# Groups of one to four small matrix products between the weight slots of the gate-up stages

## What is computed

```
def _swiglu(h, w_gu, w_down):
    gate, up = jnp.split(h @ w_gu, 2, axis=-1)
    return (jax.nn.silu(gate) * up) @ w_down        # w_down: 2816 x 1024

def _conv_glu_ffn(h, ffn_up, ffn_conv, ffn_conv_bias, ffn_down):
    u = _causal_dwconv(h @ ffn_up, ffn_conv) + ffn_conv_bias
    gate, val = jnp.split(u, 2, axis=-1)
    return (jax.nn.gelu(gate, approximate=True) * val) @ ffn_down
```

## Time and profile before

| what | value |
|---|---|
| median of 2 runs | 1998.72 us |
| lowest, highest | 1992.91, 2004.54 us |
| the profiled execution's own time | 1990.14 us |
| its span, first to last instruction | 1988.3 us |
| TensorE busy | 1886.5 us, 15758 matmuls |
| VectorE, ScalarE, GpSimd busy | 1211.8, 1002.9, 708.1 us |
| mean granted clock of TensorE | 0.974 of full speed |

### The profile page before, as it was taken

How to read it: one execution, slowest core, us unless ns; L and a number is a source line. 1 busy time by engine, 2 the same in 40 slices (tenths; PEclk the granted TensorE clock), 3 DMA queues, 4 the chain that set the end, 5 groups by cost and what they waited for, 6 DMA issues and landing times.

```text
span 1988.3 us, 41005 instructions
## 1 busy us (share of the span) xinstructions
PE 1886.5 (95%) x15758; PEld 1847.9 (93%) x15758; DVE 1211.8 (61%) x1482; ACT 1002.9 (50%) x1312; POOL 708.1 (36%) x595
## 2 busy tenths in 40 slices
PE   6999999999999999999999998997999889979997
PEld 6999999999999999999999997987999789969997
DVE  4545586666556645676665576556774665657755
ACT  5434465454354435555544456455654474546543
POOL 3761211257416621303376102513660005225630
PEclk9999999999999999999999989998999889999998
DMA  6546444456455546344454633222554433214544
GB/s 222 196 148 218 170 148 148 160 187 206 160 199 190 196 165 216 128 149 170 170 202 160 203 134 106 86 86 87 191 189 160 135 106 107 89 60 170 190 153 165
DMA packets 49225, 314.42 MB, mean 158 GB/s; under 512 B 5712, under 2 KB 6864, under 8 KB 19920
## 3 DMA queue, kind: packets, MB, share of 16 engines
q1 hardware_dynamic: 48960, 311.09, 45.5%
q10 hardware_dynamic: 144, 1.69, 0.2%
HBM read 311.71 MB, written 1.05 MB: 157 GB/s over the span
## 4 chain that ended last, share of the span: by engine, by line
PE 67%; ACT 9%; DVE 9%; DMA 7%; issue 4%; POOL 2%; SPq 0%; ACTq 0%; DVEq 0%; POOLq 0%
PE ps L546 17%; PE ps L548 17%; PE ps L547 17%; ACT w_hi L1175 5%; DMA raw<-in_down_dram 5%; DVE w_lo L1656 4%; PE ps L551 3%; PE ps L885 3%; PE ps L553 3%; PE ps L552 3%; DMA raw<-in_in_dram 1%; PE ps L696 1%; PE ps L736 1%; DVE rstd L1662 1%; DVE conv L1982 1%
## 5 line engine op out<-in xcount | busy, mean ns | idle before, releaser
L1656 DVE TENSOR_TENSOR w_lo<-raw,w_hi 128x2048 fp32r<-128x2048 f32 (+1 forms) x322 | 696.1, 2162 | 359.7 <-ACT w_hi L1175 358.3
L546 PE MATMUL ps<-xn,w_hi 128*128 128x256 f32 x2688 | 763.8, 284 | 39.5 <-DVE w_lo L1656 14.4
L547 PE MATMUL ps<-xn,w_hi 128*128 128x256 f32 x2688 | 754.1, 281 | 0.0
L548 PE MATMUL ps<-xn,w_lo 128*128 128x256 f32 x2688 | 754.0, 280 | 0.0
L1175 ACT ACTIVATE w_hi<-raw 128x2048 fp32r<-128x2048 f32 (+1 forms) x322 | 562.6, 1749 | 135.4 <-DMA raw<-in_down_dram 88.1
L546 PEld LDWEIGHTS ps<-xn,w_hi 128*128 128x128 f32 x2688 | 514.6, 191 | 48.1 <-issue 37.1
L547 PEld LDWEIGHTS ps<-xn,w_hi 128*128 128x128 f32 x2688 | 515.1, 192 | 0.7 <-issue 0.5
L548 PEld LDWEIGHTS ps<-xn,w_lo 128*128 128x128 f32 x2688 | 515.4, 192 | 0.0
L546 PE MATMUL ps<-h,w_hi 128*128 128x256 f32 x1056 | 293.1, 278 | 3.0 <-DVE w_lo L1656 2.9
L547 PE MATMUL ps<-h,w_hi 128*128 128x256 f32 x1056 | 292.5, 277 | 0.0
L548 PE MATMUL ps<-h,w_lo 128*128 128x256 f32 x1056 | 292.5, 277 | 0.0
(11 more groups left out here) (322 smaller groups left out, 2680.0 us busy)
## 6 DMA issues: line engine op xcount, KB each, us to landing
raw<-in_gu_dram SPq DMA_DIRECT2D x132, 1024.0 KB, 4.9
raw<-in_in_dram SPq DMA_DIRECT2D x70, 1024.0 KB, 4.9
raw<-in_down_dram SPq DMA_DIRECT2D x96, 704.0 KB, 4.0
raw<-in_out_dram SPq DMA_DIRECT2D x16, 1024.0 KB, 4.8
raw<-in_pb_dram SPq DMA_DIRECT2D x4, 1024.0 KB, 4.9
raw<-in_pa_dram SPq DMA_DIRECT2D x4, 1024.0 KB, 4.8
tables_all<-in_tables_dram ACTq DMA_DIRECT2D x1, 1648.0 KB, 6.9
rows<-in_rows_dram SPq DMA_DIRECT2D x2, 768.0 KB, 5.4
```

The lines of the kernel that those rows point to most:

```text
L546: pe.matmul(out, w, xh, start=first, stop=False)
L547: pe.matmul(out, w, xl, start=False, stop=False)
L548: return pe.matmul(out, wl, xh, start=False, stop=last)
L1656: dve.tensor_tensor(w_lo[:, r, 0:elems], raw[:, k % RAW_RING, 0:elems], w_hi[:, r, 0:elems], ALU.subtract).then_inc(lo.sem, 1)
```

## The change

A new helper `aside(kind, r)` issues a short group of products into bank 7 (`AUX + 1`). Their results are read by nobody. In the first block's `gate_up` a group stands ahead of each of the 20 slots in the loop, with kinds 0, 1, 2, 3 in turn. In the second block a group stands ahead of slots 1, 2 and 3 of each round in the loop, with kinds 4, 5, 7 in layer 0 and 9, 10, 11 in layer 1. Ahead of each group TensorE waits for the weights of the slot that follows; in the first block also for the tables. Kinds 6 and 8 are defined and not used.

| kind | products in the group | stationary x moving |
|---|---|---|
| 0, 1 | 2, 1 | fp32 `ones_d` x `ident`, 128 columns |
| 2, 5 | 1, 2 | fp32 `ones_d` x `rstd`, 256 columns |
| 3 | 1 | fp32r `w_hi` x `xn`, 128 columns |
| 4 | 1 | fp32r `xn` x `w_hi`, 256 columns |
| 7, 11 | 1 | fp32 `ones_d` x `ident`, 1 and 64 columns |
| 9 | 1 | fp32r `w_hi` x `xn`, 256 columns |
| 10 | 1 | fp32r `xn` x `w_hi`, 72 columns |

```diff
@@ -580,12 +580,39 @@
             s = xn_lo_even if c % 2 == 0 else xn_lo_odd
             pe.wait_ge(s.sem, s.upto(at, k * KC // 2 + c // 2 + 1))
 
+        def aside(kind, r):
+            out = ps[:, AUX + 1, 0:T]
+            if kind in (0, 1, 8):
+                for i in range((2, 1, 0, 0, 0, 0, 0, 0, 3)[kind]):
+                    pe.matmul(ps[:, AUX + 1, i * P:(i + 1) * P], ones_d[:], ident[:], start=True, stop=True)
+            elif kind in (2, 5):
+                for i in range(1 if kind == 2 else 2):
+                    pe.matmul(ps[:, AUX + 1, i * T:(i + 1) * T], ones_d[:], rstd[:, 0:T], start=True, stop=True)
+            elif kind == 3:
+                pe.matmul(ps[:, AUX + 1, 0:P], w_hi[:, r, 0:P], xn[:, 0, 0, 0:P], start=True, stop=True)
+            elif kind == 4:
+                pe.matmul(out, xn[:, 0, 0, 0:P], w_hi[:, r, 0:T], start=True, stop=True)
+            elif kind == 6:
+                pe.matmul(out, w_hi[:, r, 0:P], xn[:, 0, 0], start=True, stop=True)
+                pe.matmul(out, w_hi[:, r, 0:P], xn[:, 0, 1], start=True, stop=True)
+            elif kind == 7:
+                pe.matmul(ps[:, AUX + 1, 0:1], ones_d[:], ident[:, 0:1], start=True, stop=True)
+            elif kind == 9:
+                pe.matmul(out, w_hi[:, r, 0:P], xn[:, 0, 0], start=True, stop=True)
+            elif kind == 10:
+                pe.matmul(ps[:, AUX + 1, 0:72], xn[:, 0, 0, 0:P], w_hi[:, r, 0:72], start=True, stop=True)
+            elif kind == 11:
+                pe.matmul(ps[:, AUX + 1, 0:64], ones_d[:], ident[:, 0:64], start=True, stop=True)
+
         def gate_up(at, st, k, prev):
 
             wide(at, st, 0, 0, xn, KC, k - 1, lambda: mean_square(at, k), prev)
             wide(at, st, 1, 0, xn, KC, None, None, prev)
             with pe.Fori(0, (FC - 2) // 4) as g:
                 for j in range(2, 6):
+                    slot(at, st, j, g)
+                    pe.wait_ge(ready.sem, 16 * N_TABLES)
+                    aside(j - 2, (st.slot0 + j) % RING)
                     wide(at, st, j, g, xn, KC)
 
         def slot(at, st, j, g=0):
@@ -1117,7 +1144,13 @@
             out_part(3, 0, KC)
             mean_square(at, 0)
             mean_square_direct(at, 1)
-            cycle(pe, FC, 4, lambda j, g: wide(at, st2["gu"], j, g, xn, KC, 0))
+            def gate_up_slot(j, g):
+                if not isinstance(g, int) and j:
+                    slot(at, st2["gu"], j, g)
+                    aside(((4, 5, 7), (9, 10, 11))[layer][j - 1], (st2["gu"].slot0 + j) % RING)
+                wide(at, st2["gu"], j, g, xn, KC, 0)
+
+            cycle(pe, FC, 4, gate_up_slot)
             down(at, st2["down"], 0, st2["gu"])
             mean_square_direct(at, 2)
 
```

## The result

The changed kernel took 2035.69 us (median of two runs, 2033.44 and 2037.94) against 1998.72 before: ratio 1.0184, 95% interval 1.0143 to 1.0224. Measured again at the end beside new runs of the kernel before it was 2031.20 against 1999.36, ratio 1.0163, 1.0135 to 1.0191. So it is 32 to 37 us slower, on the near side of 2% by both medians, though the first interval reaches past it; 2032 was forecast.

The account below looks back on a forecast made before the run. TensorE, busy without gaps in the gate-up stages, was taken to bound the kernel. An all-fast base of 1983.5 us plus 32.7 of group work plus 15.5 of slow pace gave 2031.7, say 2032 us, range 2015 to 2056.

Parts of the forecast that it names:

- What bounds the kernel: Whole kernel: TensorE is busy 95% of the span, without gaps in the gate-up stages, and sets the time.
- rival 3: At all 110 groups the sequencer falls behind on waits and register work, 11 to 22 us more; chance 0.06.
- rival 4: Groups cost nothing but their effect on the pace, slipping under the loads: 1984 to 1999 us; chance 0.05.
- The work: TensorE time of the 110 groups: 24.4 us in block 1, 6.1 and 2.3 in block 2, together 32.7.
- No cover: At every group TensorE is on the chain, so the 32.7 us of products are paid in full.
- The pace by kind: Gate-up and down stages: which pace each kind leaves; 20% of block 1's matmuls slow, 75% of block 2's, 15.5 us.
- The size of the pace: Gate-up stages and down stages behind: 4.42 ns a matmul over 9024 matmuls, 39.9 us between all fast and all slow.
- The base: Whole kernel with all stages fast: profiled 1990.1 us with its one slow stage pair, 6.6 us, made fast gives 1983.5.
- I add nothing for it: No term for the median standing 8.6 us above the profiled run, read as stages falling into the other pace.
- all slow: Rival 1: most groups in the gate-up stages leave the slow pace; all slow gives 2056 us; chance 0.25.
- all fast: Rival 2: every group in the gate-up stages leaves the fast pace, 2016 us; chance 0.14.
- The mixed case: The forecast itself: groups leave mixed paces in the stages, same pattern each round, 2017 to 2038 us; chance 0.49.

Follow-up runs that it names:

- the first profile: Profiled execution of the changed kernel in its first measurement, 2033.44 us; that measurement's median was 2035.69 us against 1998.72 for the kernel before.
- the second profile: Profile of the unmodified changed kernel measured once more beside new runs of the kernel before: 2031.20 us against 1999.36, ratio 1.0163.
- the first execution: Profiled execution of the kernel before the change, from which the prediction was made: 1990.1 us, with one stage pair slow.

## Why the prediction was right, and where only its sum was

*What bounds the kernel.* Right. TensorE without gaps, no other engine in the way, and the waits added at no cost (rival 3 fell with the kernel that has waits alone; rival 4 with the prices).

*The work.* Forecast 32.7 us. By the measured prices it is 20 x (0.45 + 0.23 + 0.43 + 0.12) + 5 x (0.12 + 0.87 + 0.23) + 5 x (0.11 + 0.12 + 0.23) = 33.0 us. The choice for the one-column product, 0.23 between 0.1 and 0.25, was right. The 25 ns floor that the Trainium skill gives (TensorE: Matmul & The Clock Gate, "Wait — 56ns, not 53.3ns?") does not price a product that brings its own load; the load's price on the same page ("LDWEIGHTS"), 107 ns for 128 columns, is near the 0.11 us a record that the traces show. The early start of 0.03 us that the prediction reads from the earlier trace rows cannot be read there, since the row merges two records.

*"No cover."* Wrong in a small way. The first group of a stage in block 1 stands ahead of the wait for drained banks, and in three of the four stages it lies in it. TensorE's waits for line 1689, in the kernel before and in the changed one (where it is line 1722):

```profile
PE ps L546 <- DVE hv L1689: 4.8, 3, 2.8
```

```profile
PE ps L546 <- DVE hv L1722: 1.5, 3, 0.6
```

3.3 us less, of which at most 3 x 0.45 are kind 0 groups that cost nothing there; the rest is presumably TensorE coming later, when the banks were drained.

*The pace by kind.* The step that failed. "Kinds 0 and 1 fast, 2 and 5 keep what is there, single fp32r products keep it, the short kinds 7, 10 and 11 slow": kinds 0, 2 and 4 met fast leave slow, kind 3 changes the pace whichever it meets, kind 5 met slow left fast, and 7, 10 and 11 keep a fast stream fast. Of the matmuls counted for block 1, 20% were to be slow and about 44% were in the first profile (55 of the 80 slots behind a group, and no down stage); of those of block 2 75% were to be and 8% were (5 slots). In the second profile it was about 54 and 40%, with 57 and 5 slots and three down stages. The reasoning behind it took eight records of 128 columns for a model of four, and one case for a rule; the measured rule depends on the number of records and on the form met. The two errors had opposite signs, which is luck. Even the rounds that repeat could not have been read from the earlier trace rows, since the forms do not show in a matmul's mean.

*The size of the pace.* 4.42 ns a matmul was right, and a stage pair at 6.6 us nearly so (4.7 and 1 to 2.3). What was wrong is that a down stage keeps the pace of its gate-up stage, on which 14 of the 39.9 us rest: behind a wait near its start three of six came out slow in the second profile and none in the first. In slow matmuls the pace came to about 12.7 us in the first profile and 19.5 in the second, on either side of the 15.5 forecast.

*The base.* 1983.5 us was taken from one execution whose parts outside the stages, 872.5 us, were the shortest of all profiles taken (874 to 881 in the others). "I add nothing for it" was wrong by 3 to 8 us. In place, the change cost 34.9 us in the first profile (38.4 less 3.5), 33.0 of it work and 1.9 for pace less what the waits covered, against the 8.9 forecast for pace beyond what the first execution had; in the second it cost 42.0 (38.8 and 3.2), 9.0 beyond the work. That the sum 2032 fell within 4 us of both medians is thus partly luck: the pace differed from one execution to the next by more than that.

*The rivals.* Neither all slow nor all fast came true. The mixed case was right in kind, slow and fast slots in the same pattern in each round, but not in which kinds leave which.

## What to carry to other kernels

- Small products put into a dense stream of matmuls are paid in full, here at about 0.11 us for each fp32r record and each fp32 record of up to 128 columns, and twice that for an fp32 record of 256. One column costs what 128 do, as a load of its own would have it. Only in front of a wait that is there anyway can they vanish.
- Before explaining some tenths of a per cent of a TensorE-bound kernel, divide stretches without gaps by their matmul counts: two paces (here 113.3 and 117.75 ns) at the same clock can hold for whole stages and change between runs of the same kernel, likely at the waits ahead of them.
- What a faster stretch gives is read from where the work behind it starts, in several traces and not in one, for a wait behind it may take the gain or move along; and a base from one execution deserves a check against the median.

## What the runs showed of the hardware that was not expected

Streams of 128 x 128 loads with 256 moving fp32r columns run at 113.3 or 117.75 ns a matmul at a granted clock of 1.00. The slow pace has one load in three at 192 instead of 188 ns, in one of three forms. Each of ten kinds of interruption takes each of the forms it met, and the fast pace, to one and the same successor, 777 times of 777, where no wait follows; three of the cells rest on a single group or two. Behind a wait one and the same kernel showed either pace in two executions. A group of two one-column records keeps the fast pace or restores it from the form of 546 (14 of 14); four records of 256 columns left the fast pace in every case (38 met fast, 15 in the form of 546). Nothing here shows what in the engine holds the pattern.
